# The two weight sums of the Strassen feed-forward blocks move from VectorE to GpSimd, and refills wait one remainder longer

## What is computed

```python
def swiglu(x, w_gate, w_up, w_down):
    return (jax.nn.silu(x @ w_gate) * (x @ w_up)) @ w_down

for l in range(DEPTH_2):
    x = x + 0.5 * swiglu(rms_norm_2(x, ffn1_norm[l]), ffn1_w_gate[l], ffn1_w_up[l], ffn1_w_down[l])
    ...   # attention, merge, w_out
    x = x + 0.5 * swiglu(rms_norm_2(x, ffn2_norm[l]), ffn2_w_gate[l], ffn2_w_up[l], ffn2_w_down[l])
```

## Time and profile before

| | us |
|---|---|
| median of 3 executions | 3258.0 (3250.89 to 3263.54) |
| profiled execution | 3250.51 |
| its span in the trace | 3248.8 |
| mean granted TensorE clock | 0.948 |
| PE / VectorE / ScalarE / GpSimd busy | 90% / 56% / 46% / 22% |

### The profile page before, as it was taken

One profiled execution on the slowest core, in us unless ns is written; L12 is line 12 of the kernel. 1 busy time (PEld: TensorE's weight loads), 2 busy tenths in 40 slices (PEclk: granted clock), 3 DMA queues, 4 the chain that ended last, 5 costly groups with the idle time before them and its releaser, 6 DMA issues.

```text
span 3248.8 us, 48731 instructions
## 1 busy us (share of the span) xinstructions
PE 2921.2 (90%) x16264; PEld 2451.9 (75%) x16264; DVE 1820.7 (56%) x2469; ACT 1488.0 (46%) x2173; POOL 708.0 (22%) x353
## 2 busy tenths in 40 slices
PE   5988869996799988989999999899988979989998
PEld 3755657775599866767779988799766767779987
DVE  7544258885777334762247752877234652267743
ACT  3251337774655333653245543655234653255532
POOL 2430201110011332112421124011432113321133
PEclk8997969998899998999999999999998989999999
DMA  6610249996476231101246633566231102257623
GB/s 274 265 39 1 94 158 358 367 363 246 109 182 182 86 118 70 40 33 65 90 117 175 181 110 107 140 178 171 85 130 52 39 26 78 84 138 183 183 92 113
DMA packets 143512, 448.53 MB, mean 138 GB/s; under 512 B 13665, under 2 KB 13937, under 8 KB 141041
## 3 DMA queue, kind: packets, MB, share of 16 engines
q1 hardware_dynamic: 113136, 373.08, 32.8%
q0 software_dynamic: 28816, 63.45, 10.3%
q10 hardware_dynamic: 1456, 10.66, 0.8%
HBM read 434.55 MB, written 16.78 MB: 139 GB/s over the span
## 4 chain that ended last, share of the span: by engine, by line
PE 47%; issue 36%; POOL 7%; DVE 5%; DMA 4%; ACT 2%; POOLq 0%; SPq 0%; DVEq 0%; ACTq 0%
PE pb L1417 8%; PE pb L1418 8%; PE pb L1419 8%; POOL w_lo L483 6%; PE pb L1098 6%; PE pb L1099 6%; PE pb L1100 6%; DMA rows<-h_rows,h_idx 3%; PE pb L1105 1%; PE pb L1171 1%; DVE rs L1672 1%; DVE g_wl L2074 0%; PE pb L1226 0%; PE pb L1225 0%; PE pb L1299 0%
## 5 line engine op out<-in xcount | busy, mean ns | idle before, releaser
L483 POOL TENSOR_TENSOR w_lo<-raw,w_hi 128x1024 fp32r<-128x1024 f32 x220 | 548.0, 2492 | 1309.1 <-ACT w_hi L562 1309.1
L1417 PE MATMUL pb<-bl,g_wh 128*128 128x256 f32 x2464 | 711.8, 289 | 48.4 <-DVE bl L2124 30.0
L1418 PE MATMUL pb<-bh,g_wl 128*128 128x256 f32 x2464 | 702.0, 285 | 0.0
L1419 PE MATMUL pb<-bh,g_wh 128*128 128x256 f32 x2464 | 701.7, 285 | 0.0
L1417 PEld LDWEIGHTS pb<-bl,g_wh 128*128 128x128 f32 x2464 | 477.9, 194 | 57.4 <-DVE bl L2124 32.1
L1418 PEld LDWEIGHTS pb<-bh,g_wl 128*128 128x128 f32 x2464 | 477.9, 194 | 4.8 <-issue 4.8
L1419 PEld LDWEIGHTS pb<-bh,g_wh 128*128 128x128 f32 x2464 | 477.9, 194 | 0.0
L562 ACT ACTIVATE w_hi<-raw 128x1024 fp32r<-128x1024 f32 x220 | 231.6, 1053 | 282.1 <-PE pb L1100 267.5
L1098 PE MATMUL pb<-hl,w_hi 128*128 128x512 f32 (+1 forms) x688 | 290.0, 422 | 50.1 <-DVE hl L1683 17.3
L1098 PE MATMUL pb<-fl,w_hi 128*128 (+1 forms) x704 | 279.4, 397 | 8.8 <-DVE fl L2164 8.8
L1099 PE MATMUL pb<-bl,w_lo 128*128 128x512 f32 x704 | 279.1, 396 | 0.0
(11 more groups left out here) (366 smaller groups left out, 5360.3 us busy)
## 6 DMA issues: line engine op xcount, KB each, us to landing
raw<-in_wstream SPq DMA_DIRECT2D x220, 512.0 KB, 3.3
m_raw<-in_moe_stream SPq DMA_DIRECT2D x192, 512.0 KB, 6.3
g_own<-in_gu_stream SPq DMA_DIRECT2D x90, 512.0 KB, 5.1
raw<-in_gu_stream SPq DMA_DIRECT2D x88, 512.0 KB, 5.5
g_own<-in_gu_stream POOLq DMA_DIRECT2D x45, 512.0 KB, 5.7
raw<-in_gu_stream POOLq DMA_DIRECT2D x44, 512.0 KB, 5.8
ada_ring<-in_ada SPq DMA_DIRECT2D x8, 2048.0 KB, 7.9
g_own<-in_gu_stream SPq DMA_DIRECT2D x45, 256.0 KB, 3.5
```

The source lines that it names most:

```text
L483: pool.tensor_tensor(w_lo[s][:], raw[s][:], w_hi[s][:].bitcast(F32), ALU.subtract).then_inc(w_lod, 1)
L1417: pe.matmul(o, lh, rl, start=first and k == 0, stop=False, skip_group_check=True)
L1418: pe.matmul(o, ll, rh, start=False, stop=False, skip_group_check=True)
L1419: m = pe.matmul(o, lh, rh, start=False, stop=k == 3, skip_group_check=True)
```

## The change

`sums` moves from VectorE to GpSimd, directly behind the `add_gu` of the same block. Its waits stay as they were: loads landed, accumulating DMA landed, lo_s24 of the block before. SP's refill of the buffer of block Q-2 waits for `g_lo` 4Q+3 instead of 4Q+2, which is lo_s24 of block Q-2 and no longer lo_s31. The first load of down weights waits for 4(Q0+NF)+7 instead of +6, again lo_s24 for lo_s31, of the last block. Nothing else differs; all line numbers of VectorE's part shift.

```diff
             def load_gu(Q, u, read=None):
                 if type(Q) is not int:
-                    sp.wait_ge(g_lo, 4 * Q + 2)
+                    sp.wait_ge(g_lo, 4 * Q + 3)
...
-                    stream_pair(b0, 4 * (Q0 + NF) + 6)
+                    stream_pair(b0, 4 * (Q0 + NF) + 7)
...
+            def sums(Q, n, u):      # gpsimd
+                aa, s31 = (g_parts[u][n].rearrange("p a k m -> p a (k m)") for n in range(2))
+                pool.wait_ge(g_in[u], 32 * (n + 1))
+                pool.wait_ge(g_sum[u], 16 * (n + 1))
+                pool.wait_ge(g_lo, 4 * Q + 7)
+                pool.tensor_tensor(sq[:, 0, :], s31[:, 1, :], aa[:, 0, :], ALU.add).then_inc(g_s24, 1)
+                pool.wait_ge(g_s24, 2 * Q + 1)
+                pool.tensor_tensor(sq[:, 1, :], sq[:, 0, :], aa[:, 1, :], ALU.add).then_inc(g_s24, 1)
...
             def first_pair(Q, n):      # vector
                 lo_aa(Q, 0)
-                sums(Q, n, 0)
                 lo_s31(Q, 0)
...
                     gate_lo(Q, k, c)
                     if not last:
                         lo_aa(Q + 1, 1 - u)
-                        sums(Q + 1, n + u, 1 - u)
                     up_hi(Q, c)
```

More of the change, by code:

```diff
@@ L530, in _ @@
             add_gu(0, 0, 0)
+            sums(0, 0, 0)
             with pool.Fori(0, NL) as l:
@@ L535, in _ @@
                     add_gu(Q0 + 1, n0, 1)
+                    sums(Q0 + 1, n0, 1)
                     with pool.Fori(1, NF // 2) as i:
@@ L538, in _ @@
                             add_gu(Q0 + 2 * i + u, n0 + i, u)
+                            sums(Q0 + 2 * i + u, n0 + i, u)
                     with pool.Fori(0, n - 1) as j:
@@ L542, in _ @@
                     low_pair(b0 + n - 1)
+                    sums(Q0 + NF, n0 + NF // 2, 0)
         @block.scalar
@@ L2105, in _ @@
             lo_aa(0, 0)
-            sums(0, 0, 0)
             lo_s31(0, 0)
@@ L2200, in ffn @@
                 up_hi(Q0, 0)
-                sums(Q0 + 1, n0, 1)
                 gate_hi(Q0, 0, 0)
@@ L2207, in ffn @@
                 lo_aa(Q0 + 2, 0)
-                sums(Q0 + 2, n0 + 1, 0)
                 up_hi(Q0 + 1, 1)
```

## The result

| | before | after |
|---|---|---|
| median, executions of both in the same comparison | 3260.8 us (3250.9 to 3265.8) | 3350.1 us (3341.6 to 3360.8) |
| profiled execution | 3250.5 | 3357.2 |
| span in the trace | 3248.8 | 3355.5 |
| mean granted TensorE clock | 0.948 | 0.932 |

The changed kernel is slower by 2.8%: ratio 1.0279, 95% interval 1.0234 to 1.0324, some 89 us. The forecast was 3271 in a range up to 3288, so it was wrong by far more than its range.

What follows compares the result with a forecast made beforehand. PE was taken to bound the kernel, 100% busy in the loop. Loop 0, entries 1.7 + 3.2 + 2.6 + 3.2 and end 2.4 gave +13.1 us: 3263.6 from the profiled 3250.5, 3271 against the median; range 3257 to 3288.

Steps and rivals of the forecast that it cites:

- The loop costs nothing, 0.8 to 1.2 us to spare: Loop over the blocks: the later refill and moved additions still fit, so no time is lost.
- The chain of 18.9 us: Loop: from the refill's issue through load, landing, additions and high part to the remainder, 18.9 us against two blocks' 20.16.
- GpSimd's round, 9.3 us: Loop: landing 5.8, waiting 1.1 and additions 2.4 us make GpSimd's work per block, under the block's 10.08 us.
- Rival (a), the loop breaks: Loop: load plus landing exceed 13.4 us, overshooting two blocks by 0.65 us; 3284 us in total, chance 0.20.
- Entries and end, 13.1 us: Four SwiGLU entries and kernel's end: GpSimd's additions and VectorE block each other, delaying remainders; +13.1 us in all.
- rival (d): Entries: PE's clock also falls behind longer waits, four extra drops adding 8 us; 3279 us, chance 0.11.
- The turns: Entries and end: VectorE and GpSimd exclude each other for whole instructions and alternate; +2.4 us at the end.
- Additions at 1.2 us: GpSimd: each moved 128x512 addition takes 1.2 us, 2.4 us the pair, against 1.4 us for the pair on VectorE.
- (b): Entries: GpSimd's small additions hardly disturb VectorE, so entries cost near zero; 3258 to 3262 us, chance 0.15.
- (c): Wait after the norm: taking additions off VectorE shortens it by 1.4 us four times, 5.5 us; 3252 us, chance 0.04.

Runs made afterwards that it cites:

- experiment 7: Changed kernel with the early refill, VectorE's s31 remainder waiting for GpSimd's additions, and additions of blocks 0 and 1 back on VectorE: 3271.0 us, ratio 1.0019.
- experiment 3: Changed kernel with only the a22 load held back by one more remainder (4Q+5 instead of 4Q+4): 3283.2 us, ratio 1.0080.

## Why the prediction was wrong

**The loop costs nothing, 0.8 to 1.2 us to spare: wrong, and the step that failed.** The chain of 18.9 us took 6.3 us from load to accumulating DMA and 5.8 us for the landing as constants. Both are times of DMAs that run beside each other, and the change moves one against the other. In the changed kernel the first is 8.2 us in the median, the second up to 10.9. At 1863.11 the sum is 9.3 + 10.6 = 19.9 us, against 12.1 in the prediction. My rows held half of the warning: 8.2 us from load to DMA, and in the trace of the kernel before ten blocks in a row of f = 2 are like it (7.8 to 8.6).

**GpSimd's round, 9.3 us: too short.** I let the addition meet VectorE once. In the loop both additions can have to take turns (4.1 us for the pair in experiment 7 against 3.5), and the round fills the block. I take that to be the additions' own share in the loop; it is argued from sequences and not shown by a run.

**Rival (a), the loop breaks: the right mechanism at a fraction of its price.** I priced it as an overshoot of the chain, 0.33 us a block, 13 to 26 us. A late landing is no small overshoot but a jump of 4 us and more, which costs 7.4 us with the block behind it (74 us over ten). Its condition, load plus landing over 13.4 us, was met in those blocks. The sign that I had named for it did not come: PE waited for ScalarE's evacuations behind `hi_s31`, not for the remainder of `sq`.

**The a22 load: missed.** I wrote that behind SP's wait only the a22 load is queued, whose own wait is later still. True, but its distance to the load ahead of it shrank from 2.8 to 0.65 us, and experiment 3 shows that this is worth 67 us.

**Entries and end, 13.1 us: 18 measured, and the waits give less than half of it.** By place, predicted and measured: f = 0 1.7 and 4.0, f = 1 3.2 and 1.6, f = 2 2.6 and 3.6, f = 3 3.2 and 5.1, end 2.4 and 3.6. The sum comes near partly by luck. From the first activation remainder to block 3 the four entries grow by 12.5 us, but only 4.2 of it is idle time of PE. The other 8.3 are longer matmuls: PE is busy 172.4 us with the same 1096 of them instead of 164.1, at a granted clock of 0.85 to 0.90 instead of 0.86 to 0.96. That term I had put at nothing in the sum, and priced in rival (d) alone. PE's waits for activation remainders rise from 36.6 to 42.0 us in the whole kernel, 5.4 where I had expected about 10.

The end can be followed instruction by instruction (timelines of GpSimd and VectorE; it answers to the earlier trace rows):

```profile
3334.10 2.40 POOL L483 TENSOR_TENSOR w_lo<-raw,w_hi 128x1024 fp32r<-128x1024 f32 x1 [3.05 <-ACT w_hi L576]
3336.45 2.28 POOL L502 TENSOR_TENSOR sq<-g_own 128x512 f32<-128x512 f32 x1
3338.81 2.15 POOL L504 TENSOR_TENSOR sq<-sq,g_own 128x512 f32<-128x512 f32 x1
...
3335.00 4.81 DVE L2088 TENSOR_TENSOR g_wl<-g_own,g_wh 128x1024 fp32r<-128x1024 f32 x2 [1.21 <-ACT g_wh L816]
3342.17 1.22 DVE L2088 TENSOR_TENSOR g_wl<-sq,g_wh 128x1024 fp32r<-128x1024 f32 x1 [2.35 <-ACT g_wh L828]
...
3343.91 4.87 DVE L2233 SCALAR_TENSOR_TENSOR x<-pb,x 128x512 f32<-128x512 f32 x8
```

From the start of the last weight remainder to the x additions it is 9.81 us now and was 7.78 (3229.44 to 3237.22): +2.0, predicted 2.4. The turns are as I took them: the two additions take 2.28 and 2.15 us, and VectorE's two remainders 4.81 instead of 2.4. The other 1.5 us arise early in this down stage: PE does 19 matmuls in 7 us (3215.2 to 3222.2) instead of 26 (3112.0 to 3119.0 before), with the same idle time, at a granted clock of 0.76 instead of 1.00. What made the clock fall there, when it did not before behind the same wait, these traces do not show. It is the term of rival (d), and in the loops it took part too, 7.6 of 24 us in the window above and 29 of 89 in all. I had priced it at 8 us at most.

**Additions at 1.2 us: nearly right.** Undisturbed they take 1.29 to 1.32 us, in the mean with the turns 1.45 to 1.66 (GpSimd by form: busy us, mean ns of one):

```profile
L504 POOL TENSOR_TENSOR sq<-sq,raw 128x512 f32<-128x512 f32 x44 | 73.2, 1664 | 3.5
...
L502 POOL TENSOR_TENSOR sq<-raw 128x512 f32<-128x512 f32 x44 | 63.9, 1452 | 278.9 <-DMA raw<-in_gu_stream 227.4 <-DVE g_wl L2088 51.5
```

**Rivals (b) and (c): refuted.** The blocking is in the turns above. VectorE's relief paid nothing: PE's wait after the norm is 11.9 us in four times, as before.

## What to carry to other kernels

A DMA's duration from a trace holds only for the traffic that ran beside it, so when a change moves one DMA in time, draw both issue times of every pair that share the engines and ask which of them come together; do it too for loads that are not moved but whose predecessor is. A steady loop in which a late load makes the next one later has no margin of 1 us, whatever the sum of the chain says: ask how far it drifts. And price a wait that has been moved onto an in-order engine by what stands behind it there, here the next accumulating DMA behind two additions.

## What the runs showed of the hardware

Of an accumulating DMA from GpSimd (512 KB) and SP's loads (1 MB), whichever moved its first packet first held the other back. Alone the first packets came 1.9 and 1.0 us after the issue. With the aa load issued 1.37 us or less behind it, the accumulating DMA moved no packet for 3.0 to 5.2 us and landed after 9.0 to 10.9 us instead of 5.7, in 43 of 43 blocks; with 1.38 us or more, in none of 773. The other way round, loads issued 1.4 to 3 us behind it waited 3.1 us for their first packet. Whether the one that stands is held back in the making of its descriptors or in the DMA engines, the traces do not show, and I did not try it.

VectorE's remainders and GpSimd's additions took turns, a whole instruction each: while the remainder of 1.42 us at 1874.82 ran, the addition issued at 1875.24 took 2.13 us, 0.8 more than alone.
